# First and third normalisation of a two-layer transformer kernel: transposes tile by tile, per-block waits of the first products, order of the opening loads, place of the log table's load

## The reference

```python
def rmsnorm(x, g):
    r = rsqrt(mean(x * x, axis=-1, keepdims=True) + EPS)
    return x * r * g

# first block
h = rmsnorm(x, norm1_g);  proj = h @ w_in;  u, v_a, q, k, v_b = split(proj)
y_a = u * spatial_gating(rmsnorm(v_a));  y_b = differential_attention(q, k, v_b)
x = x + (sigmoid(h @ w_gate + b) gating y_a @ w_up_a and y_b @ w_up_b) @ w_out
x = x + hierarchical_moe(rmsnorm(x, norm2_g))          # 32 experts, 2 per token
# second block
xn = _rms(x, norm_gain_2);  proj = xn @ w_in_2
# causal convolution + silu of the first 1536 columns -> gated delta rule;
# stick-breaking attention of the next;  gates;  two up-projections;  output product
```

## Time and profile before

| | |
|---|---|
| time, median of 3 runs | 1773.82 us (1771.23 to 1778.03) |
| the profiled execution | 1772.76 us, of which the profile's span 1770.7 us |
| PE busy | 1523.5 us (86% of the span), 7159 matmuls |
| DVE busy | 948.3 us (54%) |
| ACT busy | 714.9 us (40%) |
| POOL busy | 68.2 us (4%) |
| DMA | 224.01 MB, mean 127 GB/s |

### The profile page before, as it was taken

How to read it: one execution, slowest core, us unless ns; L and a number is a source line. 1 busy time by engine, 2 the same in 40 slices (tenths; PEclk the granted TensorE clock), 3 DMA queues, 4 the chain that set the end, 5 groups by cost and what they waited for, 6 DMA issues and landing times.

```text
span 1770.7 us, 17596 instructions
## 1 busy us (share of the span) xinstructions
PE 1523.5 (86%) x7159; PEld 1147.0 (65%) x7159; DVE 948.3 (54%) x1301; ACT 714.9 (40%) x1043; POOL 68.2 (4%) x80
## 2 busy tenths in 40 slices
PE   5999997798786963899999991989697899999999
PEld 4888775586565842555555551868585877678887
DVE  3444246623763445788888874675545535321334
ACT  4333334424443220666666662244322215652231
POOL 1000000000000000111011101000000000000000
PEclk9999998998997986899999996999897988999999
DMA  6422221122104430999999984220101003002241
GB/s 197 168 96 75 96 73 66 68 75 72 70 26 161 152 119 23 307 327 340 331 336 335 329 294 156 72 71 26 47 1 48 1 24 119 1 1 72 95 143 48
DMA packets 80348, 224.01 MB, mean 127 GB/s; under 512 B 9044, under 2 KB 10182, under 8 KB 76167
## 3 DMA queue, kind: packets, MB, share of 16 engines
q1 hardware_dynamic: 71558, 193.73, 32.3%
q0 software_dynamic: 6144, 20.71, 3.5%
q10 hardware_dynamic: 2560, 8.39, 1.3%
HBM read 200.00 MB, written 22.81 MB: 126 GB/s over the span
## 4 chain that ended last, share of the span: by engine, by line
PE 59%; DVE 25%; ACT 11%; DMA 2%; issue 2%; SPq 1%; POOL 0%; DVEq 0%; POOLq 0%; ACTq 0%
PE PS L502 14%; PE PS L504 14%; PE PS L503 14%; DVE wlo L1152 7%; DVE htlo L1152 5%; PE PS L928 4%; ACT whi L1950 3%; PE PS L499 3%; DVE ylo L1152 2%; ACT work L1950 2%; PE PS L1077 2%; ACT yhi L1950 2%; PE PS L1068 1%; ACT hthi L1950 1%; DVE work L1561 1%
## 5 line engine op out<-in xcount | busy, mean ns | idle before, releaser
L1152 DVE TENSOR_TENSOR wlo<-raw,whi 128x2048 fp32r<-128x2048 f32 x74 | 169.1, 2291 | 356.3 <-ACT whi L1950 356.3
L1950 ACT ACTIVATE whi<-raw 128x2048 fp32r<-128x2048 f32 x74 | 141.2, 1912 | 334.9 <-PE PS L504 333.5
L499 PE MATMUL PS<-consts,work 128*128 128x128 f32 (+1 forms) x652 | 100.7, 298 | 125.9 <-DVE work L1178 53.2
L502 PE MATMUL PS<-whi,hthi 128*128 128x512 f32 x480 | 200.1, 417 | 9.2 <-ACT work L1950 6.4
L502 PE MATMUL PS<-hthi,whi 128*128 128x512 f32 x480 | 198.3, 413 | 5.1 <-ACT scratch L1950 2.8
L503 PE MATMUL PS<-wlo,hthi 128*128 128x512 f32 x480 | 190.9, 398 | 0.0
L504 PE MATMUL PS<-whi,htlo 128*128 128x512 f32 x480 | 190.8, 398 | 0.0
L504 PE MATMUL PS<-hthi,wlo 128*128 128x512 f32 x480 | 190.0, 396 | 0.0
L503 PE MATMUL PS<-htlo,whi 128*128 128x512 f32 x480 | 189.5, 395 | 0.0
L499 PEld LDWEIGHTS PS<-consts,work 128*128 128x128 f32 (+1 forms) x652 | 85.2, 182 | 155.1 <-DVE work L1178 54.4
L1950 ACT ACTIVATE work<-PS 128x512 f32<-128x512 f32 (+3 forms) x204 | 103.3, 531 | 88.6 <-PE PS L992 51.2
(11 more groups left out here) (320 smaller groups left out, 2600.3 us busy)
## 6 DMA issues: line engine op xcount, KB each, us to landing
raw<-in_w_in SPq DMA_DIRECT2D x44, 1024.0 KB
raw<-in_w SPq DMA_DIRECT2D x80, 512.0 KB
scratch<-in_w SPq DMA_DIRECT2D x48, 512.0 KB
raw<-in_w SPq DMA_DIRECT2D x19, 1024.0 KB
scratch<-in_w SPq DMA_DIRECT2D x13, 1024.0 KB
raw<-in_w_gate SPq DMA_DIRECT2D x8, 1024.0 KB
raw<-in_w_out SPq DMA_DIRECT2D x8, 1024.0 KB
y_scratch<-work ACTq DMA_DIRECT2D x32, 256.0 KB, 7.1
```

The source lines that it names most:

```text
L499: return e.transpose(o, i, ident[0:n, 0:n])
L502: e.matmul(o, lh, rh, start=start, stop=False)
L1152: tt(lo, raw_place(j), as_f32(hi), SUB).then_inc(*ve.mark("lo", j))
L1950: return e.activation(o, i, f, bias=bias, scale=scale)
```

## The change

On PE, n1 and n3 transpose tile by tile: the eight transposes of a tile wait for that tile alone, and a bank is complete only with the fourth tile. Of step 3, DVE makes three tiles and ACT the fourth, by a copy with scale. The first products (`va` and `qa`) wait for each block's `htlo` instead of the eighth.

At the start, ACT issues the first eight of the column loads itself, ahead of its squares; SP issues the other nine, then the first three weight units, then `wba` and the nine row loads, which now have a landing signal of their own (waited for by PE ahead of the router's bias and by DVE ahead of the lambdas); units 3 and 4 follow. DVE's copy of the gain columns moves behind the three tiles of step 3.

On ACT, the log table is loaded at the very start, and at the head of each normalisation's squares where another set is in. At n3, unit B is split ahead of the normalisation on both engines, and the first round of the `blk` loop splits two units instead of three.

The diff, cut to its core (left out: the declaration of the signal `row_got`, and `act` calling `use`):

```diff
@@ build @@
-    column_loads = []
+    column_loads, EARLY = [], 8
...
@@ tensor @@
+        def normalise_by_tile(tag):
+            on.wait_ge(*po["ident"])
+            for k in range(KD):
+                bank.take((tag, k))
+            for i in range(NT):
+                on.wait_ge(*(ve[tag, "xs", i] if i < NT - 1 else ac[tag, "xs", i]))
+                for k in range(KD):
+                    if i == 0:
+                        on.wait_ge(*emptied(bank.before[tag, k]))
+                    m = turn(PS[:, bank.of[tag, k], i * P:i * P + P], xs[:, i, k * P:k * P + P])
+                    if i == NT - 1:
+                        m.then_inc(*pe.mark(tag, k))
+                        bank.filled((tag, k))
...
-        normalise("n1")
+        normalise_by_tile("n1")
...
-            product("va", b, False, hthi, htlo, h_ready)
+            product("va", b, False, hthi, htlo, by_k=lambda k: ve["out", "n1", k])
...
         router(KD - 1)
+        on.wait_ge(*row_got["all"])
...
-        normalise("n3")
+        normalise_by_tile("n3")
...
-            product("qa", blk, True, hthi, htlo, h_ready)
+            product("qa", blk, True, hthi, htlo, by_k=lambda k: ve["out", "n3", k])
@@ vector @@
             r = inverse_rms(tag, NT, D)
+            ve.also("inverse", tag)
             settle()
-            for i in range(NT):
-                ts(xs[:, i, :], s[:, i, :], r[:, i:i + 1], None, MUL).then_inc(*ve.mark())
+            for i in range(NT if tag == "n2" else NT - 1):
+                ts(xs[:, i, :], s[:, i, :], r[:, i:i + 1], None, MUL).then_inc(*ve.mark(tag, "xs", i))
             ve.also(tag, "xs")
...
-        on.wait_ge(*pe["vectors"])
-        e.tensor_copy(vcols, inside("vectors")[:, 0:P]).then_inc(*ve.mark("out", "vectors"))
-        settle()
-        normalise("n1", g1, [split])
+
+        def gain_columns():
+            on.wait_ge(*pe["vectors"])
+            e.tensor_copy(vcols, inside("vectors")[:, 0:P]).then_inc(*ve.mark("out", "vectors"))
+            settle()
+
+        normalise("n1", g1, [gain_columns, split])
         split()
...
+        on.wait_ge(*row_got["all"])
         for n, (a, c) in enumerate((("lq1", "lk1"), ("lq2", "lk2"))):
...
+        split()
         normalise("n3", g3)
...
         for blk in range(3):
             split()
             split()
-            if blk == 0:
-                split()
@@ scalar @@
+        LOGS = "natural_log_exp_and_others"
+
+        def use(tables):
+            if tables != table[0]:
+                table[0] = tables
+                e.preload_act_table_set(tables)
...
         def normalise(tag, gains, ready, before=()):
             s = tiles(m_all[:, :])
+            use(LOGS)
...
             if tag != "n2":
+                on.wait_ge(*ve["inverse", tag])
+                act(xs[:, NT - 1, :], s[:, NT - 1, :], ACT.Copy, scale=stat[tag][1][:, NT - 1:NT]).then_inc(
+                    *ac.mark(tag, "xs", NT - 1))
                 on.wait_ge(*ve["out", "vectors"])
...
+        use(LOGS)
+        on.wait_ge(*ve["rows"])
+        for place, src in column_loads[:EARLY]:
+            e.dma_start(place, src).then_inc(*vec_got.mark())
         normalise("n1", g1, lambda i: x_got[i][i], [split])
...
+        use(LOGS)
+        split()
         normalise("n3", g3, lambda i: ve["x2", NT - 1])
...
         for blk in range(3):
             split()
             split()
-            if blk == 0:
-                split()
@@ sync @@
         on.wait_ge(*ve["rows"])
-        for place, src in column_loads + row_loads:
+        for place, src in column_loads[EARLY:]:
             e.dma_start(place, src).then_inc(*vec_got.mark())
         vec_got.also("all")
+        for j in range(NR):
+            load(j)
         e.dma_start(wba, W_IN2[:, B_A:B_A + NB].rearrange("(k p) n -> p k n", p=P)).then_inc(*ba_got.mark("all"))
-        for j in range(NR + NS):
+        for place, src in row_loads:
+            e.dma_start(place, src).then_inc(*row_got.mark())
+        row_got.also("all")
+        for j in range(NR, NR + NS):
             load(j)
```

More of the change, by code:

```diff
@@ L374, in build @@
     x_got = [landing(f"x_tile{i}") for i in range(NT)]
-    vec_got, ba_got, ws_got, yz_put, wr_got, gate_got, xw_got, xn_put, x2_put, x2_got, out_put = (
-        landing(n) for n in ("vectors", "ba", "spatial", "zeros", "router", "gate", "xw", "xn", "x2", "x2w", "out"))
+    vec_got, row_got, ba_got, ws_got, yz_put, wr_got, gate_got, xw_got, xn_put, x2_put, x2_got, out_put = (
+        landing(n) for n in ("vectors", "rows", "ba", "spatial", "zeros", "router", "gate", "xw", "xn", "x2", "x2w", "out"))
     raw_got = [landing(f"raw{s}") for s in range(NR + LENT_RAW)]
@@ L1941, in settle @@
             on.wait_ge(*ac.now())
[L1943 to L1948 removed]
+        LOGS = "natural_log_exp_and_others"
[3 more added lines that the diff above has]
+                e.preload_act_table_set(tables)
+        def act(o, i, f, bias=0.0, scale=1.0, accum_out=None):
+            need = {ACT.Exp: LOGS, ACT.Ln: LOGS, ACT.Sigmoid: "sigmoid_and_others"}.get(f)
+            if need:
+                use(need)
             if accum_out is None:
```

7 lines of the change are left out of this document (1 added, 6 removed).

## The result

| | before | changed |
|---|---|---|
| median (runs) | 1775.92 us (4, 1771.23 to 1784.81) | 1759.67 us (4, 1755.44 to 1761.97) |
| the profiled execution | 1772.76 us, span 1770.7 | 1761.97 us, span 1760.1 |
| PE busy | 1523.5 us | 1530.3 us |

The ratio is 0.990, with a 95% interval of 0.9855 to 0.9945: 0.9% faster, 16.3 us between the medians. A later comparison, on another chip, gave 0.9869 (0.9835 to 0.9903), 1755.43 us for the changed kernel. The forecast was 1758.5 us and 15.4 us less.

The account below looks back on a forecast made before the run. PE was taken as the bound, gains coming where it waits: opening 10.0 + n2 1.3 + n3 4.1 = 15.4 us, so 1772.76 becomes 1757.4; with 1.1 for the median, 1758.5 us (range 1754.0 to 1764.5).

Parts of the forecast that it names:

- The opening's start shift (8.65): At n1, the first pass of the first product starts at 18.95 instead of 27.60 us, 8.65 us earlier.
- the slack of 2.7 us: At n1, ACT's fourth tile is ready at 14.4, 2.7 us ahead of its need, hiding unit 0's split and the copy.
- Blocks as they come (0.25): In a first product, four blocks wait for `htlo` each 0.75 us against 0.68 of passes; costs 0.25 us.
- The clock in the opening (1.6): At the first product, the 1.2 GHz stretch after PE's idle time goes away; gains 1.6 us.
- The other bound, 0: Lower bound of the opening's clock gain: 0 instead of the 1.6 us counted.
- n2 (1.3): At the second normalisation, the table load moves into ACT's wait ahead of the squares; gains 1.3 us.
- the drain: The Trainium skill's 1.38 us beyond a table load's 1.28; by it each of three loads taken off would give 2.7 us.
- The rival of a dearer load: Each of three table loads also holds up work around it for 1.28 us; 1754.7 us, chance 0.03.
- n3 (4.1): At the third normalisation, first pass at 1103.15 instead of 1107.49, 4.3 us, less 0.25 for the blocks: 4.1 us.
- upper bound of 4.4: Upper end of the n3 gain, whose bounds were 3.6 and 4.4 us.
- the 25th transpose: At n3, the fourth tile's first transpose, completing the first bank, ends at 1101.3, with the first tile starting at 1095.46.
- That the transposes lift the clock: At n1 and n3, transposes raise PE's clock before the products; rival that they do not: 1761.7 us, chance 0.05.

Follow-up runs that it names:

- a_whole_wait: Changed kernel, but the two first products (n1, n3) wait for the eighth `htlo` again instead of each block; 1778.34 us in one execution.
- e_late_tables: Changed kernel with the log table loaded by the first Ln that needs it, as before, at all three normalisations; 1765.78 us in one execution.
- f_warm: Changed kernel plus throw-away transposes on PE ahead of the real ones at n1 and n3; ratio 0.9875 to the kernel before, profiled execution 1762.12 us.
- b_bank_by_bank: Changed kernel with the transposes of n1 and n3 bank by bank again, products still waiting block by block; 1758.55 us in one execution.
- g_warm_three: f_warm plus 45 throw-away transposes ahead of the second normalisation; ratio 0.9864 to the kernel before, profiled execution 1760.47 us.
- c_small_first: Changed kernel with all 26 small loads on SP ahead of the first weight unit again, none issued by ACT; 1766.88 us in one execution.
- before_third: The kernel before, unedited, profiled a third time; 1774.54 us.
- before_again: The kernel before, unedited, profiled a second time; 1768.04 us.
- after_timed: The changed kernel, unedited, timed again against the kernel before; ratio 0.9869, profiled execution 1754.98 us.

## Why the prediction came out right

The time came out at 1759.67 us where 1758.5 was forecast, and most steps of the path are where the prediction has them. Part of the hit is luck: over three profiles each the lead at the end is 13.4 us, 2 less than forecast, and the medians show 16.3, of which some 14 are the change's own work (the last part of this section).

**The opening's start shift (8.65).** The means of three profiles each are 27.21 and 19.28: 7.93 us. The forecast start was the first profile's 27.60, which lies 0.4 above the mean, and the new start came 0.3 later than 18.95. In the first profile the path was as worked out: mean 10.00 (forecast 9.85), first tile 11.27 (11.1), first transposes 12.08 (11.9). In the two others x's last tile landed later (squares from 9.19 and 9.51), and the first tile was at 11.64 and 11.96, on the mean 0.5 later than forecast; the transposes took less time and gave 0.2 of it back. In the kernel before the same scatter of x's landing (8.38 to 9.39) was hidden behind the gains' copy; the change has put it on the path. The 7.93 us are 3.4 at the mean's start, 1.28 from there to the first tile, and 3.3 from the tile to the first pass (10.94 to 7.66). The 3.4 is put down to the gains' copy, which had stood ahead of the mean; that is read from DVE's order, not from a run that puts it back. Unit 0 was there at 12.36 and not at 11.4, the fourth tile at 15.31 and not at 14.4; the slack of 2.7 us covered it, for it was needed at 17.5. ACT's issues took 0.29 to 0.59 each and ended at 4.35, not at 5.5: the forecast set them behind the table load, and they ran beside it. That gained nothing, because the squares wait for x anyway (the last from 8.82, against 8.58 before).

**Blocks as they come (0.25).** The five block starts are 19.43, 20.20, 20.90, 21.60 and 22.28; four blocks of 0.68 would end at 22.15: 0.13 us. `htlo` keeps 0.66 and not 0.75. The prediction said that this wait costs little but not what it saves; a_whole_wait shows that with the new order of transposes the wait for the eighth would have cost 4.6 and 4.7 us and a low stretch each time.

**The clock in the opening (1.6).** The size was right and its certainty not: a low stretch follows the idle time in two of three profiles of the kernel before (first and third), in none of three of the changed one. On the mean of three the lead grows by 1.05 us there, from 7.93 to 8.98. The other bound, 0, was also a measured value. So the opening gave 9.0 us where 10.0 was forecast. Nor does an idle time have to come first: some 25 us behind the first pass, where PE goes without a gap from eight small transposes and four products of one row to the passes of `u` 0, a low stretch of about 3.4 us lies in the first two profiles of the changed kernel (from 45.1 and 44.6 us on) and in the second and third of the kernel before. That the start of the product is at full clock doesn't mean that its neighbours are.

**n2 (1.3) and the drain.** The lead on the mean of three goes from 9.50 at the first square to 10.78 at the first tile: 1.28. e_late_tables has 1.28 for each of the three loads. The rival of a dearer load falls.

**n3 (4.1).** First tile to first pass 7.3 us (mean of three) instead of 10.7, and the table load 1.28: 4.7 us at the first pass, where the prediction had 4.34 before it took off 0.25 for the blocks. That is above its upper bound of 4.4. The mis-sized terms are `htlo` (0.66 instead of 0.75) and the 25th transpose, which ended 5.5 us after the first tile's start (at 1090.28, by `hthi`'s start at 1090.58 less 0.3) and not 5.84.

**That the transposes lift the clock.** At n3 32 transposes took 5.71, and passes start at full clock behind them; in f_warm real transposes behind throw-away ones run at 0.12 from the start. In the changed kernel's first profile the granted clock at n3 is 0.50 from 1085.5 to 1089.4 and 0.91 on the mean over the rest of the transposes. This speaks against the Trainium skill's rule ("TensorE: Matmul & The Clock Gate", Part 4) that transposes don't engage the full clock: PE did nothing but transposes in both places, and the pace went from some 0.21 us to 0.12.

**What the prediction lacked: the last 2 us.** It took the lead at the first pass of n3 for the lead at the end. On the mean of three profiles it is 14.9 there, close to the 15.4 forecast, 15.1 at `qa` 2's first pass, 13.5 nineteen passes on, and 13.4 at the end. So the low stretch at the start of `qa` 2 is a loss of 1.6 us, in all three profiles of the changed kernel. Nothing in the profiles says why the same idle time of 2.84 us is followed by the lower level in one kernel and not in the other, and this stays open. It doesn't come with an earlier n3 as such: b_bank_by_bank has its first pass at 1093.70 and the window behind the same idle time at 1.00. It goes with the transposes tile by tile in nine profiles out of ten; the tenth, e_late_tables, has that order and full clock (1.00 from 1146.3 to 1150.7).

**Why the medians differ by more than the profiles.** 16.3 us in the first comparison, 13.4 on the mean of three profiles, whose spans lie up to 6.5 (before) and 7.0 us (changed) apart. The executions whose span and clock are on record (37 of the kernel before, 11 of the changed) give a mean span of 1773.3 us at a mean granted clock of 0.9218, and 1755.6 at 0.9246. A straight line through the 37 falls by 1.4 us for each 0.001 of clock. At a clock of 0.924 both lines stand at 1770.2 and 1756.4: 13.8 us. So some 14 us are the change's own work, and the rest is that the kernel before had more executions at a low clock. Whether the change brings that about too, or the chips did, these runs can't say.

## What to carry to other kernels

Where a product follows a normalisation, let it wait for each block it reads and not for the last one. At n3 that was worth 2.4 us with the transposes bank by bank and 4.7 with the transposes tile by tile, where it also kept TensorE from an idle gap of 5.4 us and the low clock behind it; the order of the transposes was worth 1.0 on top and was a loss without it. Put a table load in front of a wait that is there anyway; it costs exactly its duration on the path, and nothing in a gap. And once a kernel is at the level where 0.2% counts, read a change at marks inside the profile, and take several profiles of each kernel: the 3 us that f_warm and g_warm_three gained at their marks can't be seen in their times, and the transposes of n1 alone took 5.19 to 6.57 us in one and the same kernel.

## What the runs showed of the hardware that I had not expected

- ACT's queue issues transfers while its function table is loading: the first at 1.12, the load from 0.82 to 2.10. An issue takes 0.29 to 0.59 us there, 0.25 to 0.29 on SP for the smallest.
- An issue can stand for 6 us behind large transfers. SP in the opening of the changed kernel, after three loads of 1 MB and `wba`:

```profile
8.09 5.98 SPq L2599 DMA_DIRECT2D smalls<-in_norm_g  x1
```

  The next issue is at 14.11 and took 0.29. The same issue took 5.45 and 5.49 us in the other two profiles, and 0.36 in c_small_first, where it stands ahead of the large loads. It cost nothing, for nobody waits for the row loads ahead of the first products; a load that is on the path would be late by it (an estimate, from the 5.98 us).
- The granted clock's stretches are not the same in two profiles of one kernel: the first product of the kernel before begins at 0.43 us a pass in two profiles (before and before_third, after idle times of 1.88 and 2.18 us) and at 0.23 in before_again, after 2.67.
- With less idle time ahead of the passes, TensorE was granted less clock in what followed in the profiles of f_warm and g_warm_three (0.92 over the last stretch, against 0.94 in after_timed). That the clock took the gain is what one profile of each shows, and both are of executions above the median of their kernel.
